# A hybrid decoder step on one core: all state updates of a head in groups of four, the last two groups a unit later, and the convolution taps dealt anew over the units

## The reference

```python
    h = rms_norm(x, g_mix_pre)
    proj = h @ w_in
    q, k, v, g_ret, ca, cb, ga, gb = jnp.split(proj, offs, axis=-1)
    ...
    q = rope(q.reshape(B, T, N_RET_HEADS, RET_DK), pos)
    k = rope(k.reshape(B, T, N_RET_HEADS, RET_DK), pos) * (RET_DK ** -0.5)
    ...
        cross = jnp.einsum('bihd,bhde->bihe', qc, r) * q_decay[None, :, :, None]
        r_new = r * chunk_decay[None, :, None, None] + jnp.einsum(
            'bjhd,bjhe->bhde', kc * k_decay[None, :, :, None], vc)
    ...
    o = layer_norm(o, ret_gn_gain.reshape(N_RET_HEADS, RET_DV))
    ...
    y_ret = (jax.nn.silu(g_ret) * o) @ w_ret_out
    u = ca * jax.nn.sigmoid(cb)
    padded = jnp.concatenate([c0.astype(u.dtype), u], axis=1)
    z = lax.conv_general_dilated(
        padded, conv_w[:, None, :].astype(u.dtype), window_strides=(1,), padding='VALID',
        dimension_numbers=('NWC', 'WIO', 'NWC'), feature_group_count=D_CONV) + conv_b
```

## Time and profile before

| | us |
|---|---|
| median of 3 runs | 1512.53 |
| lowest and highest | 1508.40, 1513.88 |
| profiled execution, its own time | 1511.91 |
| its span, from the first to the last instruction | 1509.9 |
| TensorE busy | 1475.3 (98%) |
| VectorE busy | 1129.1 (75%) |
| ScalarE busy | 678.2 (45%) |
| GpSimd busy | 277.6 (18%) |

### The profile page before, as it was taken

The page is one execution under the profiler, slowest core; times in us unless marked ns, Lnnn a source line. Parts: engine busy times, 40 slices in busy tenths (PEclk is TensorE's granted clock), DMA queues, the critical chain, the costliest instruction groups (busy, mean ns, idle before and its releaser), DMA issues.

```text
span 1509.9 us, 25440 instructions
## 1 busy us (share of the span) xinstructions
PE 1475.3 (98%) x9772; PEld 1382.9 (92%) x9772; DVE 1129.1 (75%) x1749; ACT 678.2 (45%) x996; POOL 277.6 (18%) x257
## 2 busy tenths in 40 slices
PE   8999999999999999999999999999999999999997
PEld 8997978888999899999999979788799998999997
DVE  6999999989666567875468897978785766666544
ACT  5343534446454444343343434445454544444433
POOL 5991211120300002556100001122011000000000
PEclk9999999999999999999999999999999999999999
DMA  8447665855545254445445465857644442544443
GB/s 330 140 152 264 237 245 184 321 185 196 166 141 186 89 167 142 150 140 180 155 144 197 161 237 196 306 191 284 226 170 148 140 142 92 170 154 140 157 163 110
DMA packets 64538, 275.46 MB, mean 182 GB/s; under 512 B 7232, under 2 KB 7232, under 8 KB 55232
## 3 DMA queue, kind: packets, MB, share of 16 engines
q1 hardware_dynamic: 52560, 192.17, 38.3%
q0 software_dynamic: 11888, 82.05, 14.5%
HBM read 230.30 MB, written 43.89 MB: 182 GB/s over the span
## 4 chain that ended last, share of the span: by engine, by line
PE 81%; DVE 10%; DMA 4%; ACT 3%; issue 2%; DVEq 0%; ACTq 0%
PE bank L456 24%; PE bank L458 23%; PE bank L457 23%; DVE state L1170 2%; DMA state<-r_in 2%; DVE acc L1139 2%; DVE wlo L1104 2%; DMA rs_out<-state 1%; PE bank L615 1%; PE bank L654 1%; PE bank L476 1%; PE bank L477 1%; PE bank L478 1%; PE bank L596 1%; DVE x L1466 1%
## 5 line engine op out<-in xcount | busy, mean ns | idle before, releaser
L456 PE MATMUL bank<-hhi,whi 128*128 128x320 f32 x2016 | 649.5, 322 | 1.9 <-DVE wlo L1104 1.9
L1104 DVE TENSOR_TENSOR wlo<-wring,whi 128x1024 fp32r<-128x1024 f32 x363 | 483.3, 1335 | 188.5 <-ACT whi L839 159.9
L458 PE MATMUL bank<-hhi,wlo 128*128 128x320 f32 x2016 | 623.8, 309 | 0.0
L457 PE MATMUL bank<-hlo,whi 128*128 128x320 f32 x2016 | 623.3, 309 | 0.0
L456 PEld LDWEIGHTS bank<-hhi,whi 128*128 128x128 f32 x2016 | 379.2, 188 | 22.9 <-issue 21.8
L457 PEld LDWEIGHTS bank<-hlo,whi 128*128 128x128 f32 x2016 | 379.5, 188 | 8.8 <-issue 7.7
L458 PEld LDWEIGHTS bank<-hhi,wlo 128*128 128x128 f32 x2016 | 379.0, 188 | 0.0
L839 ACT ACTIVATE whi<-wring 128x1024 fp32r<-128x1024 f32 x264 | 277.2, 1054 | 212.1 <-PE bank L458 211.6
L1139 DVE SCALAR_TENSOR_TENSOR acc<-up,par,acc 128x256 f32<-128x256 f32 x480 | 210.2, 505 | 0.3
L865 ACT ACTIVATE whi<-wring 128x1024 fp32r<-128x1024 f32 x96 | 101.2, 1054 | 61.6 <-PE bank L458 58.1
L456 PE MATMUL bank<-fhi,whi 128*128 128x320 f32 x352 | 110.6, 314 | 0.0
(11 more groups left out here) (174 smaller groups left out, 1888.3 us busy)
## 6 DMA issues: line engine op xcount, KB each, us to landing
wring<-w SPq DMA_DIRECT2D x364, 512.0 KB, 3.7
state<-r_in POOLq DMA_DIRECT2D x32, 1024.0 KB, 8.4
rs_out<-state POOLq DMA_DIRECT2D x32, 1024.0 KB, 5.0
rp_out<-pst POOLq DMA_DIRECT2D x8, 512.0 KB, 9.3
us<-c_in POOLq DMA_DIRECT2D x2, 1216.0 KB, 5.5
cs_out<-us POOLq DMA_DIRECT2D x2, 1216.0 KB, 8.7
cp_out<-up POOLq DMA_DIRECT2D x2, 1144.0 KB, 5.6
con<-consts POOLq DMA_DIRECT2D x1, 1421.0 KB, 9.6
```

What stands on the lines that cost most here:

```text
L456: pe.matmul(bank[g][:, 0:T], whi[j][:, k, :], hi, start=start and k == 0, stop=False)
L457: pe.matmul(bank[g][:, 0:T], whi[j][:, k, :], lo, start=False, stop=False)
L458: mm = pe.matmul(bank[g][:, 0:T], wlo[j][:, k, :], hi, start=False, stop=stop and k == n - 1)
L1104: return dve.tensor_tensor(dst, value, hi.bitcast(F32), ALU.subtract)
```

## The change

All four groups are now issued in fours. In heads that another head follows, q2 moves to (5,0) and q3 to (5,6); in the gate stage they stay at (4,3) and (5,3). The fourth products of q2 and q3 also go to bank 3: q2's waits for the rotation (or the gate's sigmoid) that reads bank 3, and unit 7 waits until q3's is read. VectorE's updates of q2 and q3 move from units 4 and 5 to 5 and 6, the transposes from unit 7 to units 7 and 8, the gated outputs all to unit 8. The taps are dealt anew. Cut to its core:

```diff
-HEAD_TAPS = ((5, 0, 3, 0, 3, 1, 5, 3, 3, 0, 0, 2), (7, 0, 3, 0, 4, 0, 5, 4, 3, 0, 0, 2), (6, 0, 3, 0, 3, 0, 3, 2, 2, 0, 0, 0))
-GB_TAPS = ((6, 0, 3, 3, 3, 1, 4, 0), (5, 0, 3, 3, 2, 1, 3, 0))
-RET_TAPS = ((2, 2, 2, 2, 0, 0), (1, 2, 2, 1, 0, 0))
+HEAD_TAPS = ((6, 0, 3, 0, 2, 3, 0, 2, 2, 1, 3, 3), (7, 0, 3, 0, 2, 3, 0, 3, 2, 1, 3, 3), (5, 0, 3, 0, 0, 2, 0, 1, 1, 1, 3, 3))
+GB_TAPS = ((6, 0, 3, 4, 3, 1, 4, 0), (5, 0, 3, 3, 2, 1, 3, 0))
+RET_TAPS = ((2, 2, 2, 2, 1, 0), (1, 2, 2, 1, 0, 0))
...
-MAIN_AS_AUX = (A_U + 3, A_U + 7)
+MAIN_AS_AUX = (A_U + 3, A_U + 7, A_U2 + 3, A_U2 + 7)
...
-QUERY_AT = ((1, 0), (1, 7), (4, 3), (5, 3))
-QUAD_AT = ((1, 0), (1, 7))
-UPDATE_AT = ((4, 3), (4, 5), (5, 3), (5, 5))
+QUAD_AT = ((1, 0), (1, 7), (5, 0), (5, 6))
+QUAD_AT_END = ((1, 0), (1, 7), (4, 3), (5, 3))
+UPDATE_UNITS, UPDATE_UNITS_END = (1, 5, 6), (1, 4, 5)
-BACK_AT = ((7, 2), (7, 3), (7, 4), (7, 5))
+BACK_AT = ((7, 6), (7, 7), (8, 0), (8, 1))
+BACK_AT_END = ((7, 2), (7, 3), (7, 4), (7, 5))
...
+                if pos == MAIN_AS_AUX[2] and H % HEADS < HEADS - 1:
+
+                    pe.wait_ge(rope_step, (H + 1) * ROPES + 10)
+                    return
+                if pos == MAIN_AS_AUX[2]:
+
+                    pe.wait_ge(sig_done, H // HEADS * SIGS + (SIG_GB + 4))
+                    return
...
-                if at in QUERY_AT:
-                    late_query(l, hd, QUERY_AT.index(at))
-                if at in QUAD_AT:
-                    late_update(l, hd, QUAD_AT.index(at), 0, QUAD)
-                if at in UPDATE_AT:
-                    late_update(l, hd, 2 + UPDATE_AT.index(at) // 2, UPDATE_AT.index(at) % 2)
+                quads, backs = (QUAD_AT, BACK_AT) if hd < HEADS - 1 else (QUAD_AT_END, BACK_AT_END)
+                if at in quads:
+                    late_query(l, hd, quads.index(at))
+                    late_update(l, hd, quads.index(at))
...
                         pe.wait_ge(rope_step, H * ROPES + (3, 4, 9, 10)[j - 4])
+                        if j == 7 and not first:
+
+                            aux_bank_free(H - 1, 3)
...
-                if j in (1, 4, 5):
-                    q = (1, 4, 5).index(j)
+                at = UPDATE_UNITS if hd < HEADS - 1 else UPDATE_UNITS_END
+                if j in at:
                     for i in range(2):
-                        update(l, hd, (0, 8, 12)[q] + i)
-                if j == 5:
-                    token_stats(l, hd, 1, range(2, 3))
-
-                    dve.wait_ge(bn_done, (l * HEADS + hd) * 3 + 3)
+                        update(l, hd, (0, 8, 12)[at.index(j)] + i)
+                if j == at[2]:
+                    sample_rows(l, hd)
...
-                    if j == 7 and not first:
-                        for e in range(3):
+                    if j == 8 and not first:
+                        for e in range(4):
                             gated_output(l, hd - 1, e)
-                    if j == 8 and not first:
-                        gated_output(l, hd - 1, 3)
```

More of the change, by code:

```diff
@@ L528, in aux_free, with aux_bank_free @@
                     pe.wait_ge(dve_aux, H * AUX_DVE + (n + 1))
-            def aux_bank_free(H):
-                pe.wait_ge(dve_aux, H * AUX_DVE + (READER[MAIN_AS_AUX[1]][1] + 1))
+            def aux_bank_free(H, q):
+                pe.wait_ge(dve_aux, H * AUX_DVE + (READER[MAIN_AS_AUX[q]][1] + 1))
             def early(l, hd, j, first=False):
@@ L618, in late_query, with late_update @@
                     mm.then_inc(stat_done, 1)
-            def late_update(l, hd, q, half, n=2):
+            def late_update(l, hd, q):
                 H = l * HEADS + hd
-                pos = (A_U, A_U + 4, A_U2, A_U2 + 4)[q] + 2 * half
+                pos = (A_U, A_U + 4, A_U2, A_U2 + 4)[q]
                 if pos == A_U:
                     pe.wait_ge(dve_aux, H * AUX_DVE + 5)
-                for i in range(n):
+                for i in range(QUAD):
                     aux_free(H, pos + i)
                 d, g = q % 2, q // 2
-                for i in range(n):
-                    row = slice((2 * half + i) * 32, (2 * half + i + 1) * 32)
+                for i in range(QUAD):
+                    row = slice(i * 32, (i + 1) * 32)
                     pe.matmul(ring(pos + i)[:, :], kst[row, g, d * P:(d + 1) * P], vst[row, g, :],
@@ L664, in late @@
                     late_within(l, hd)
-                if at in QUERY_AT:
-                    late_query(l, hd, QUERY_AT.index(at))
-                if at in QUAD_AT:
-                    late_update(l, hd, QUAD_AT.index(at), 0, QUAD)
-                if at in UPDATE_AT:
-                    late_update(l, hd, 2 + UPDATE_AT.index(at) // 2, UPDATE_AT.index(at) % 2)
+                quads, backs = (QUAD_AT, BACK_AT) if hd < HEADS - 1 else (QUAD_AT_END, BACK_AT_END)
+                if at in quads:
+                    late_query(l, hd, quads.index(at))
+                    late_update(l, hd, quads.index(at))
                 if at in PROMPT_STATE_AT:
                     late_prompt_state(l, hd, PROMPT_STATE_AT.index(at))
-                if at in BACK_AT:
-                    late_back(l, hd, BACK_AT.index(at))
+                if at in backs:
+                    late_back(l, hd, backs.index(at))
             def head(l, hd, first):
@@ L687, in head @@
                         if j == 3:
-                            aux_bank_free(H - 1)
+                            aux_bank_free(H - 1, 1)
                     elif j < 8:
                         pe.wait_ge(rope_step, H * ROPES + (3, 4, 9, 10)[j - 4])
+                        if j == 7 and not first:
+                            aux_bank_free(H - 1, 3)
                     else:
@@ L732, in _ @@
                         if n == 3:
-                            aux_bank_free(l * HEADS + HEADS - 1)
+                            aux_bank_free(l * HEADS + HEADS - 1, 1)
                     else:
                         pe.wait_ge(sig_done, l * SIGS + (SIG_GB + n - 3))
+                        if n == 7:
+                            aux_bank_free(l * HEADS + HEADS - 1, 3)
                     u = U_GB + n
@@ L1171, in update, with sample_rows @@
                                          op0=ALU.mult, op1=ALU.add).then_inc(dve_aux, 1)
+            def sample_rows(l, hd):
+                token_stats(l, hd, 1, range(2, 3))
+                dve.wait_ge(bn_done, (l * HEADS + hd) * 3 + 3)
             def first_updates(l, hd, j):
-                if j in (1, 4, 5):
-                    q = (1, 4, 5).index(j)
+                at = UPDATE_UNITS if hd < HEADS - 1 else UPDATE_UNITS_END
+                if j in at:
                     for i in range(2):
-                        update(l, hd, (0, 8, 12)[q] + i)
-                if j == 5:
-                    token_stats(l, hd, 1, range(2, 3))
-                    dve.wait_ge(bn_done, (l * HEADS + hd) * 3 + 3)
-                if j == 6:
+                        update(l, hd, (0, 8, 12)[at.index(j)] + i)
+                if j == at[2]:
+                    sample_rows(l, hd)
+                if j == 6 and hd == HEADS - 1:
                     token_shift(l, hd, 1, slice(2, 3))
             def updates(l, hd, j):
-                if j == 5:
+                at = UPDATE_UNITS if hd < HEADS - 1 else UPDATE_UNITS_END
+                if j == at[2]:
                     token_mean_var(range(2, 3))
-                if j in (1, 4, 5):
-                    q = (1, 4, 5).index(j)
+                if j in at:
                     for i in range(2, QUAD):
-                        update(l, hd, (0, 8, 12)[q] + i)
+                        update(l, hd, (0, 8, 12)[at.index(j)] + i)
                 if j == 1:
@@ L1196, in updates @@
                         update(l, hd, QUAD + i)
+                if j == 6 and hd < HEADS - 1:
+                    token_shift(l, hd, 1, slice(2, 3))
             def token_stats(l, hd, n, chunks):
```

## The result

The changed kernel takes 1514.83 us (median of 8 runs, 1513.85 to 1519.88) against 1511.99 for the kernel before on the same chip (1508.12 to 1514.52). The ratio is 1.0031, 95% interval 1.0020 to 1.0042: some 3 us slower, inside the range and inside the band of no change. It is the value of rival 1. The profiled execution took 1515.24 us, 3.33 more than that of before.

A forecast was written before the change was run, and what follows sets the result against it. TensorE, busy 98% of the span, was taken as the bound, so only gaps between its matmuls could be won. Base 1511.9 plus terms gave 1514.8, and three clock falls (+4.6) 1519.4; predicted 1519, range 1508 to 1527.

The forecast's parts named there:

- rival 1: Waits before group 3 and unit 7 come but TensorE's clock holds: 1514.8 us, chance 0.22.
- the sum without clock: Base 1511.9 plus 1.6, 0.1, -2.7, 1.2, 0.8 and 1.9 for the kernel's parts: 1514.8 us.
- Windows of the six heads: Unit 4 to unit 7, set by VectorE's chain: 17.27 us in layer 0 (+1.6 in all), 15.82 in layer 1 (+0.1).
- the release: From VectorE's last step to TensorE's start: 0.14 us, plus 0.08 for the first triple after a wait.
- Gate stages: Both gate stages: fours for twos save the whole 1.36 us in each, -2.7 in all.
- The bound of -1.4: Gate stages: the total if TensorE gives half the saving back waiting for the normalised tokens.
- Gated outputs in unit 8: Transposes behind unit 8 wait for banks the gated outputs free: 0.2 us a head, +1.2; bounds 0 and 8.8.
- The tap ahead of the stacked values: One more tap before group 0's last update in two first-layer heads: 0.4 us each, +0.8.
- The retention stage: Layer 0, unit 4: a tap moved there delays GpSimd's add and TensorE's mean, +1.9 us; lower bound 0.8.
- The clock: A fall of TensorE's clock, 1.54 us, behind each of the three longest waits: +4.6; bounds none and 10.8.
- Rival 2: Slower: the clock falls behind all seven waits, in six heads and the retention stage: 10.8 us, 1525.6; chance 0.33.
- Rival 3: Faster: VectorE isn't the gate and TensorE passes unit 4 to 7 at 13.80 in all six heads: 1494.4; chance 0.04.

The follow-up runs named there:

- e1: The changed kernel with no tap of a head left in units 4 and 5; they go to unit 6: 1510.29 us, ratio 1.000 to the kernel before.
- e4: The changed kernel with the three tap tables of the kernel before put back: 1522.21 us, ratio 1.0068 to the kernel before.
- e7: The changed kernel with GpSimd's add of the third channel pair moved earlier in the gate stage: 1513.78 us, ratio 1.0019 to the kernel before.
- e10: The kernel before, groups 2 and 3 in twos, with e8's taps and moved GpSimd add: 1507.46 us, ratio 0.9965 to the kernel before.
- e2: The changed kernel with groups 2 and 3 of the heads at (4,3) and (5,3), updates in units 4 and 5: 1513.13 us, ratio 1.0009.
- e5: The kernel before with only the three tap tables of the change: 1512.27 us, ratio 1.0008 to the kernel before.
- e6: The changed kernel, layer 0's last tap moved from the retention stage's unit 4 to the gate stage's unit 7: 1516.59 us, ratio 1.0029.
- e8: Changed kernel with fours at (4,3) and (5,3), the earlier tail, taps dealt anew and GpSimd's add moved: 1499.58 us, ratio 0.9927 to the kernel before.
- e9: e8 with one tap of unit 0 moved into unit 1 in layer 0's third and fourth heads: 1499.31 us, ratio 0.9907 to the kernel before.

## Why the prediction came out as it did

The predicted time, 1519, was 4 us too high; the terms other than the clock's were right within 1.2 us each, and the sum without clock, 1514.8, is the measured median. So what came is rival 1 with a single fall, not the forecast with three. That the sum meets the median is partly luck. Without its one fall (1.56) the profiled execution would have taken 1513.7, 1.1 below the sum, and in the sum errors cancel: the windows, the gated outputs and the retention stage came out 0.9, 0.8 and 1.2 better than forecast, the gate stages and the waits at (1,7) 1.1 and 0.5 worse.

- **Windows of the six heads.** Forecast 17.27 and 15.82, measured 17.11 and 15.68. The order of the steps was right, and e1 shows that it is this chain that counts. Oversized was the release, 0.22: VectorE ends at 162.65 and unit 7 starts at 162.75, 0.10. In e4 the same working failed by 0.7 in layer 1, where the taps no longer covered the way from VectorE's read to TensorE's next products and back.
- **Gate stages.** Forecast -1.36 each. Layer 1: -1.30. Layer 0: -0.36. The step that failed is "whose chain on ScalarE starts from unit 5 and comes earlier by as much": it came earlier, right into GpSimd's add. e7 shows it. TensorE's wait before the transposes grew from 0.94 to 1.77 us, and 0.34 came at unit 7. The agreement in layer 1 is partly luck: there the same wait grew from 0.94 to 1.55, and the queries' wait for their state happened to be shorter (0.37 instead of 1.03). The 1.36 itself was a little too big: e10 gives 1.21. The bound of -1.4 for both was for this kind of loss, and the sum -1.66 lies within the bounds.
- **Gated outputs in unit 8.** Forecast +1.2, got +0.4. That they cost little here holds only as long as TensorE is late itself: in e1 and e2 they cost 3.6 and 5.9.
- **The tap ahead of the stacked values.** Forecast 0.4 in two heads, got 0.17, 0.47 and, unforeseen, 0.66 in the gate stage. There VectorE, and beside it GpSimd with a sample tap and a sum of channels, show:

```profile
310.10 1.73 DVE L1117 TENSOR_TENSOR wlo<-wring,whi 128x1024 fp32r<-128x1024 f32 x1
311.76 4.75 DVE L1152 SCALAR_TENSOR_TENSOR acc<-up,par,acc 128x256 f32<-128x256 f32 x6
```
```profile
310.83 2.11 POOL L332 TENSOR_TENSOR acc<-us,stap 128x512 f32<-128x512 f32 x1
313.08 1.55 POOL L379 TENSOR_TENSOR pairs<-acc 128x640 f32<-128x640 f32 x1
```

  The six tap instructions take 4.75 instead of 2.46: the moved taps met GpSimd's adds, 2.3 us in all. But in the kernel before the same two adds met two small steps of VectorE, which took 1.38 and 1.79 us where they now take 0.35 and 0.40, 2.4 in all, so the collision is not new, and it is not shown to be the cause of the 0.66. What is shown is that the deal of taps makes these waits: e4, with the old tables, has none at (1,7), and e5, with the new ones, has 0.40 and 0.58.
- **The retention stage.** Forecast +1.9 with the bound 0.8, got 0.70. The delay was right: the add behind the last tap starts 17.55 us after the stage's first matmul (369.49 to 387.04) against 15.63 before (365.45 to 381.08), 1.92 later. That there is no room was nearly right too, since the mean then waits 0.55 for GpSimd. The mis-sized term is the length of the add, which took 2.50, not 3.63; the bound of 0.8 for that case was close. The prediction ties that length to an add that meets no low half, but this one meets two. Now, then before:

```profile
387.04 2.50 POOL L379 TENSOR_TENSOR pairs<-pairs,acc 128x640 f32<-128x640 f32 x1 [27.02 <-DVE acc L1152]
```
```profile
386.88 1.22 DVE L1117 TENSOR_TENSOR wlo<-wring,whi 128x1024 fp32r<-128x1024 f32 x1
...
388.52 2.10 DVE L1117 TENSOR_TENSOR wlo<-wring,whi 128x1024 fp32r<-128x1024 f32 x1
```
```profile
380.92 2.35 DVE L1104 TENSOR_TENSOR wlo<-wring,whi 128x1024 fp32r<-128x1024 f32 x2
```

  Before, two low halves stand one right behind the other at the start of the add; now the first has a step that reads a bank behind it, and it is the second that takes longer, 2.10 instead of 1.22. In e6, with the tap gone, the add takes 3.62 again, so the 0.70 is 1.9 of delay less 1.1 of the add. The same add takes 1.56 in the gate stage. No run moved a low half alone.
- **The clock.** Forecast three falls, got one in the profile. The profiles of e6 and e7, which leave the heads of layer 0 as they are, have two each: 5 falls at 9 waits of 2.24 us, and none at the nine waits of 1.44 in layer 1. So the failed step is to take every one of the three longest waits for a fall: by these profiles the number to expect is 3 x 5/9 = 1.7, not 3. Rival 2, a fall behind all seven, is refuted. The runs of the change go from 1513.85 at a mean clock of 0.998 to 1519.88 at 0.994: that is where its spread comes from.

Rival 3, windows of 13.80, was refused for the right reason, VectorE's durations, but these hold for one order alone: e8 reaches 13.88.

## What to carry to other kernels

When a helper engine is the gate, write its chain down to the next engine that waits for it, and then on to the second and the third: an edit that shortens the first wait (e1, e2, e5) moves it to the next thing that this engine owes, and the gain arrives only when the whole tail moves too. Work that fills the way there and back between two engines costs nothing (0.76 us of it here, e4); the same work anywhere else in the chain costs all of it. If a stage that should have gained didn't, look for one instruction there that takes ten times its usual time. And count the falls of the clock in both profiles before comparing them.

## What the runs showed that was not expected

- TensorE's clock fell to its lower level at waits of 1.03 us, 1.77, 1.87, 2.45 and 2.46 (e4), 1.90 (e2) and 2.24 us, and in e9 behind 1.13 and 0.41 close together (at 507.59 and 509.55), in a stage that the change doesn't touch. It held at 1.12, 1.66, 1.92, 2.00 and others of 1.77 and 2.24. None of the nine waits of 1.44 had a fall and five of the nine of 2.24 had one, so the length of a wait alone doesn't decide it; what else does is not shown. A fall cost 1.4 to 1.6 us where nothing else held TensorE behind it. In e4 the one at 1.87 made its head only 0.8 longer, because the wait of 0.71 before unit 7 went with it, and the one at 2.46 lasted twice as long as the others.
- A VectorE instruction of 0.15 us took 1.56 beside a GpSimd add of 1.56 (0.77 in layer 1, where the two overlapped for less), and it was on the critical path because the units ahead of it had become 1.3 us shorter (15.13 us from unit 4 to unit 7 of the gate stage, against 16.39).
- A wait of TensorE for the load of a state (0.25 to 1.9 us at the first queries of group 2) varies from profile to profile: 0.78 us in the gate stage of layer 0 in the change, 1.13 in e6, which is the same kernel up to there. In e8 it takes 0.40, 1.10 and 0.57 us in three of the six heads; removing it was not tried.
